# The sums of weights in a Strassen-like feed-forward block, made in the pair that uses them

## The reference, cut to what matters

```
x = x + mix @ w_out                      # rg_out in layer 0, sb_out in layer 1
h = rmsnorm(x, norm_ffn_g[layer])
g = h @ w_gate                           # 1024 x 2816
u = h @ w_up                             # 1024 x 2816
x = x + (silu(g) * u) @ w_down           # 2816 x 1024
```

## Time and profile before

| | |
|---|---|
| median of 3 runs | 1966.46 us (1963.02 to 1968.39) |
| the profiled execution | 1964.4 us, span 1962.7 us |
| TensorE busy | 1875.2 us, 96% of the span |
| VectorE busy | 1279.7 us, 65% |
| ScalarE busy | 951.7 us, 48% |
| mean granted TensorE clock | 0.988 |
| DMA | 208.64 MB, mean 106 GB/s |

### The profile page before, as it was taken

One profiled execution on the slowest core, in us unless ns is written; L12 is line 12 of the kernel. 1 busy time (PEld: TensorE's weight loads), 2 busy tenths in 40 slices (PEclk: granted clock), 3 DMA queues, 4 the chain that ended last, 5 costly groups with the idle time before them and its releaser, 6 DMA issues. The chain is left out here.

```text
span 1962.7 us, 30196 instructions
## 1 busy us (share of the span) xinstructions
PE 1875.2 (96%) x10662; PEld 1567.3 (80%) x10662; DVE 1279.7 (65%) x2220; ACT 951.7 (48%) x1573; POOL 233.6 (12%) x322
## 2 busy tenths in 40 slices
PE   9999888998899999988899899999999999999998
PEld 7787788888888777778898898876677887777777
DVE  7787767646765766677764676666677556556553
ACT  6576556325544444556632454345565344445442
POOL 3011111001100000011100110000001135341000
PEclk9999999999999999989999999999999999999999
DMA  7334566346532222256634653212222233232322
GB/s 253 104 97 129 144 154 153 103 122 167 123 106 75 66 64 64 65 149 152 150 108 120 165 123 120 76 54 59 62 84 76 94 88 89 75 91 75 96 82 74
DMA packets 79220, 208.64 MB, mean 106 GB/s; under 512 B 10209, under 2 KB 18529, under 8 KB 79121
## 3 DMA queue, kind: packets, MB, share of 16 engines
q1 hardware_dynamic: 60080, 174.16, 28.3%
q0 software_dynamic: 19040, 33.20, 9.7%
HBM read 203.12 MB, written 4.21 MB: 106 GB/s over the span
## 5 line engine op out<-in xcount | busy, mean ns | idle before, releaser
L642 PE MATMUL ps<-Hl,Wh 128*128 128x512 f32 x784 | 328.4, 419 | 0.0
L1340 ACT ACTIVATE Wh<-Wr 128x1024 fp32r<-128x1024 f32 (+2 forms) x172 | 195.6, 1139 | 257.4 <-PE ps L644 232.9
L644 PE MATMUL ps<-Hh,Wh 128*128 128x512 f32 x784 | 307.2, 392 | 0.0
L643 PE MATMUL ps<-Hh,Wl 128*128 128x512 f32 x784 | 306.4, 391 | 0.0
L1903 DVE TENSOR_TENSOR Wl<-Wr,Wh 128x1024 fp32r<-128x1024 f32 (+2 forms) x172 | 231.4, 1345 | 102.9 <-ACT Wh L1340 101.6
L642 PE MATMUL ps<-Yl,Wh 128*128 128x512 f32 (+1 forms) x648 | 253.9, 392 | 11.4 <-DVE Wl L1903 8.2
L643 PE MATMUL ps<-Yh,Wl 128*128 128x512 f32 (+1 forms) x648 | 250.4, 386 | 0.0
L644 PE MATMUL ps<-Yh,Wh 128*128 128x512 f32 (+1 forms) x648 | 250.2, 386 | 0.0
L728 PE MATMUL ps<-Hl,Wh 128*128 128x256 f32 x528 | 155.3, 294 | 58.2 <-DVE gs L2096 57.3
L642 PEld LDWEIGHTS ps<-Hl,Wh 128*128 128x128 f32 x784 | 147.4, 188 | 40.3 <-issue 11.3
L644 PEld LDWEIGHTS ps<-Hh,Wh 128*128 128x128 f32 x784 | 147.1, 188 | 32.9
(11 more groups left out here) (404 smaller groups left out, 4106.5 us busy)
## 6 DMA issues: line engine op xcount, KB each, us to landing
Wr<-in_w SPq DMA_DIRECT2D x162, 512.0 KB, 3.6
Wr<-in_w SPq DMA_DIRECT2D x32, 768.0 KB, 4.1
scr<-in_w SPq DMA_DIRECT2D x66, 256.0 KB, 3.3
Wr<-in_w SPq DMA_DIRECT2D x66, 256.0 KB, 3.0
scr<-in_w SPq DMA_DIRECT2D x22, 512.0 KB, 5.0
scr<-in_w POOLq DMA_DIRECT2D x44, 256.0 KB, 6.5
Wr<-in_w POOLq DMA_DIRECT2D x44, 256.0 KB, 5.7
Wr<-in_w SPq DMA_DIRECT2D x16, 640.0 KB, 3.8
```

The costliest lines, as they stand in the source:

```text
L642: pe.matmul(bank[:, 0:n], hi, rl[:, k, :], start=(k == 0), stop=False)
L643: pe.matmul(bank[:, 0:n], lo, rh[:, k, :], start=False, stop=False)
L644: return pe.matmul(bank[:, 0:n], hi, rh[:, k, :], start=False, stop=(k == kc - 1))
L1340: act.activation(place(Wh, slot, kc), place(Wr, slot, kc), ACT.Copy).then_inc(w_hi, 1)
```

## The change

Four things:

- `second_sum(g)` and `fourth_sum(g)` are made at the beginning of pair g (behind the rest of S4 of g-1 and behind the rest of S3 of g+1), where before those of g+1 were made in the middle and at the end of pair g.
- The cast and the rest of S2 of pair g are made in pair g, ahead of those of A of g+1, where before S2 of g+1 came last in pair g. Pair 0 keeps its place: its sums are made in `out_proj` and in the first iteration.
- `split_at` numbers the stream to match; the waits of SP, TensorE, ScalarE and VectorE that use it follow.
- In `out_proj` of `rg_out` and `sb_out`, at m = 3, 4 and 5, the rest of the weight two units on goes ahead of the row quarters, where before it came behind them.

```diff
 def split_at(h, pairs):
+    at = {"S3": 6 * h - 2, "A": 6 * h, "A22": 6 * h + 2, "S2": 6 * h + 5, "S1": 6 * h + 7, "S4": 6 * h + 9}
     if isinstance(h, int) and h == 0:
-        return {"S3": 1, "A": 2, "A22": 3, "S2": 4, "S1": 7, "S4": 10}
+        at.update(S3=1, A=2, A22=3, S2=4)
+    if isinstance(h, int) and h == 1:
+        at.update(S3=5)
     if isinstance(h, int) and h == pairs - 1:
-        return {"S3": 6 * h - 1, "A": 6 * h, "A22": 6 * h + 2, "S2": 6 * h + 3, "D0": 6 * h + 5, "S1": 6 * h + 6, "S4": 6 * h + 7}
-    return {"S3": 6 * h - 1, "A": 6 * h, "A22": 6 * h + 2, "S2": 6 * h + 3, "S1": 6 * h + 7, "S4": 6 * h + 10}
+        at.update(S2=6 * h + 4, D0=6 * h + 5, S1=6 * h + 6, S4=6 * h + 7)
+    return at
...
# ScalarE, ffn_in, iteration(g, par)
-                    used = {..., "S2": 6 * g + 3, "S4": 6 * g - 2}
+                    used = {..., "S2": 6 * g - 3, "S4": 6 * g - 2}
...
                     if drain:
                         return
+                    if n != 0:
+                        sum_hi(name, g, "S2", par, b + used["S2"])
                     if n == 0 and norm:
                         root(norm)
                     if more:
...
                     if more:
                         sum_hi(name, g + 1, "A22", 1 - par, b + used["A22"])
-                        sum_hi(name, g + 1, "S2", 1 - par, b + used["S2"])
...
# VectorE, out_proj
                     if name in ("rg_out", "sb_out") and m == 0:
                         split(u0 + 4, 0, KD)
+                    if pairs_in and nrm and 2 < m < 6:
+                        split(u0 + m + 2, m % 2, KD)
                     if pairs_in and nrm and m % 2 == 0:
                         even_quarters(nrm, m)
                     if pairs_in and nrm and m % 2:
...
-                    elif (m > 2 or name not in ("rg_out", "sb_out")) and m < 6 or not pairs_in:
+                    elif not nrm and m < 6 or not pairs_in:
                         split(u0 + m + 2, m % 2, kc_of(u0 + m + 2))
...
# VectorE, ffn_in, iteration(g, par)
                     if n != 0:
                         sum_lo(name, g - 1, "S4", 1 - par)
+                    if n != 0 and not drain:
+                        second_sum(name, g, par)
                     if n not in (0, 1) and not drain:
                         act_by_up(g - 2, par)
                     if more and n != 0:
                         sum_lo(name, g + 1, "S3", 1 - par)
+                    if n != 0 and not drain:
+                        fourth_sum(name, g, par)
                     if n not in (0, 1):
                         y_lo_ffn(g - 2, par)
...
                         sum_lo(name, 1, "S3", 1)
+                    else:
+                        sum_lo(name, g, "S2", par)
                     if more:
-                        second_sum(name, g + 1, 1 - par)
                         sum_lo(name, g + 1, "A", 1 - par)
...
-                    if more:
-                        fourth_sum(name, g + 1, 1 - par)
-                        sum_lo(name, g + 1, "S2", 1 - par)
```

More of the change, by code:

```diff
@@ L1441, in iteration @@
                     more = n is None or n + 1 < pairs
-                    used = {"S3": 6 * g - 1, "A": 6 * g, "S1": 6 * g + 1, "A22": 6 * g + 2, "S2": 6 * g + 3, "S4": 6 * g - 2}
+                    used = {"S3": 6 * g - 1, "A": 6 * g, "S1": 6 * g + 1, "A22": 6 * g + 2, "S2": 6 * g - 3, "S4": 6 * g - 2}
                     if n == 0:
-                        used = {"S3": 2, "A": 2, "S1": 0, "A22": 3, "S2": 4}
+                        used = {"S3": 2, "A": 2, "S1": 0, "A22": 3}
                     if n == 1:
-                        used["S4"] = 0
+                        used.update(S2=4, S4=0)
                     if last:
```

## The result

The changed kernel takes 1894.89 us, median of 4 runs (1893.74 to 1895.18), beside 1965.15 for the kernel before on the same chip (4 runs, 1963.02 to 1968.39). The ratio is 0.9641, 95% interval 0.9625 to 0.9656: faster by 3.6%. The prediction was 1890.5 us, range 1883 to 1908: the forecast case came true, 4.4 us above its number. The profiled execution took 1895.13 us, its span is 1893.5, where the kernel before had 1964.4 and 1962.7.

A forecast was written before the change was run, and what follows sets the result against it. A DMA leg and VectorE's in-order queue, closing in one turn of the pair loop, were taken as the bound: 1964.4 - 75.8 + 2.2 - 2.4 = 1888.4, given as 1890.5 since the runs' median is 2.1 higher; range 1883 to 1908.

The forecast's parts named there:

- the forecast case: Whole kernel: TensorE becomes the bound at 10.06 us a turn; 1890.5 us, alone spanning 1884 to 1898; chance 0.72.
- The loop and its new length: Gate/up pair loop through `sum1`: 12.32 us in one turn before, 15.6 us over two after, 7.8 a turn.
- VectorE's clock: Gate/up pair: VectorE's instructions timed from TensorE's S3 at 0, 8.2 us of work within 10.06, 0.6 us left over.
- the prediction's own sign of being wrong: Changed profile: TensorE waits for the rest of S2 or A, or accumulates land later than 7 us after issue.
- Gain 75.8: Four gate/up stretches: 439.0 us fall to 363.2, as 36 turns of 10.06 plus twice 0.5 us.
- 0.5 us for the norm: Pair 1 of the two norm stages: 0.5 us each for the norm's spread, added to the stretches.
- Loss 2.2: Stage ends: down's unit 0 loads later, costing 1.0 us in each of two stages, 0.1 in the others.
- Gain 2.4: Out-projection at m = 3: the weight's rest moves up 1.2 us, in two places; 0 to 8.2 possible.
- "0" for the quarters: Out-projection at m = 4 and 5: row quarters, now later, stay hidden behind TensorE's units, costing 0.
- its case: Pair loop: VectorE's row of waits becomes the bound; at 10.5 us a turn it loses 16 us: 1906; chance 0.14.
- The DMA case: Pair loop: the DMA leg still shows; an accumulate of 12 us gives 10.7 a turn, 1914; chance 0.08.
- the 19 us from which I had the change turn slower: Slower rival: leg through `sum1` must pass 19 us instead of 10.24; at 21 us, 2000; chance 0.04.

## Why the prediction was right, point by point

- **The loop and its new length: right.** The wait of 93.4 us is 0.6; the steady turn is 10.07 for 10.06. The 12.2 us a turn that the prediction set out from is an average that no usual turn had, pair 1 at 15 to 18.5 and the others at 11.6; the sum is not hurt by it, since it starts from the whole stretches. Taking the leg away (10.07 in the old order) and lengthening it (one turn pays all, two turns pay the excess) show the cause, not only its end.
- **VectorE's clock: right to 0.2 us.** From S3 at 1056.54: second sum 1.47 (1.6 predicted), fourth 3.27 (3.4), low part of Y 4.34 (4.4), the instruction behind S2's rest 5.89 (6.05), second read to 9.3 (9.4).
- **DMA: right for S1, wrong for S3.** S1: load at 8.08 (8.0), landing 17.0 (17.6), sum 21.61 (21.7). The load of S1 is slower than in the earlier trace rows and the accumulate faster (4.2 for 5.7), so that the leg kept its length while its parts changed. S3 was to land "within a microsecond of S1's"; it lands 4.4 us later in the turn shown, and 3.2 to 4.7 in most. Its accumulates take 7.4 us at the median where they took 6.5, so that the prediction's own sign of being wrong, accumulates that land later than 7 us after their issue, was there. That the time held all the same was partly luck: the 4 us of room are S1's alone, and the cast of S3 has half a microsecond at the median. The engines' share is 0.66 to 0.68, not 0.72; with the sums at the end of the pair before it is 0.69 to 0.72. Why stays open.
- **"Gain 75.8": 72.7.** The term that I mis-sized is pair 1 and pair 2 of the two norm stages. Pair 1's turn is 11.63 and 11.53, not 10.56. It also has two matmuls of 512 columns that no other pair has (0.46 us), a delay of about 0.5 at a read, and one of about 0.3 for the rest of S2, each followed by a few slower starts. Without the accumulate, in the order of before, it is 11.53 as well, so it is no DMA and none of the change's doing: I had 0.5 us for the norm where 1.5 were due. Pair 2 is 10.44 and 10.58, 0.4 and 0.5 us where I took 0 and had 1.4 as the bound; without the accumulate it is 10.07. Not the buffer that I looked at shows there: the second sum waits only 0.19 us and stands at 246.65. It is S3 of pair 3, whose late landing holds ScalarE, and through its cast VectorE's queue ahead of the rest of S2:

```profile
248.75 0.63 ACT L1377 ACTIVATE Fh<-scr 128x512 fp32r<-128x512 f32 x1 [1.07 <-DMA scr<-in_w]
```

  The prediction's own sum had less room there than it said, too: from 247.29, six instructions and the rest of S2 end at 251.3 by its start-to-start times, not at 250.8, with TensorE wanting it at 251.5.
- **"Loss 2.2": 4.2.** The mechanism is as put: load at 3.49 after S3 (3.5 predicted), TensorE idle for 1.04 and, at the third stage's end, 0.81. But I followed unit 0 alone. The load of unit 1 is later too (12.5 us after the last S3 for 10.8), its rest comes ahead of the right rows, and Y with it: another 0.5 us in each of the two longer stages. In the two shorter ones down's first matmul comes at 10.36 and 10.45 after the last S3, not 10.06, where I had put 0.1. With the last pair's sums made early all of it is gone from the first stage (87.27 for 89.00).
- **"Gain 2.4": 2.3 in the two profiled executions (2.22 and 0.12), and not to be told from 0 in the medians.** The idle at m = 3 fell by 1.3 at each place, as the edit says. The step that failed is "0" for the quarters: they are hidden at m = 4 and 5, but pair 0 waits for them, 1.34 us in `sb_out` where there was no wait, 1.29 in `rg_out` where there were 0.77. In `rg_out` the clock did not fall in this execution (below), as it did in that of before; how much of the 2.22 is the clock's stays open.
- **The sum.** 76.0 predicted (75.8 - 2.2 + 2.4), 69.3 measured between the two profiled executions. The 6.7 are: stretches 3.1, ends 2.0, units 0.1, and 1.7 ahead of anything edited, for which a prediction has no term.
- **The rivals.** VectorE had over 1.2 us to spare and less than 2.4; its case was further off than the 0.6 left over on my clock said. The DMA case was priced by the right formula but with a leg that grows only in the accumulate; in the kernel with two accumulates the load grows as well (4.59), and so the leg is dearer. A leg of 17.77 gave 1958, still under the kernel before: that fits the 19 us from which I had the change turn slower. VectorE without pauses (50.00 of 50.00) did not hold up POOL's issues, 0.88 us each at the median as before (0.87). By that, the trace agrees with the Trainium skill (SBUF — State Buffer, "Who interferes with whom"), which takes tensor_tensor for harmless to GpSimd's descriptors.

## What to carry to other kernels

Where an engine waits in its queue for a DMA although the DMA engines are half idle, write down the loop: from the instruction that frees the buffer, over load and accumulate, to the one that uses it, and through the queue back to the freeing one; the length of the loop by the turns that it spans is the bound. If it binds, move the waiting instruction to behind the instruction that frees the next buffer: any place will do between the landing and the use, and the latest is not the best, for what the moved instruction frees (here down's first load) moves along with it. After such a move, follow the next stage's first two loads, not only the first, and every other DMA that shares the queue: here S1's leg kept over 4 us of room and S3's, behind it, 0.5. And look at the first turns of such a loop by themselves: a third of the gain lay in four turns of 36.

## What the runs showed of the hardware

- **Two idle moments of nearly the same length, one with and one without a fall of the clock.** At the same unit of two stages of the kernel after, on its timeline of TensorE:

```profile
204.64 0.47 PE L645 MATMUL ps<-Yl,Wh 128*128 128x512 f32 x1 [2.78 <-DVE Wl L1907]
...
804.21 0.77 PE L645 MATMUL ps<-Yl,Wh 128*128 128x512 f32 x1 [2.86 <-DVE Wl L1907]
```

The 8 us behind each, by stretch:

```profile
204.64:212.64 8.00, 8.00 (x35) 6.61 (x36) 7.05 (x12) 4.63 (x6) 0.93 (x1) 1.00 0.83 263
804.21:812.21 8.00, 8.00 (x28) 6.53 (x29) 7.05 (x12) 4.29 (x6) 0.87 (x1) 0.79 0.72 222
```

Full speed in the first, a part of the time at 1.2 GHz in the second. Over all kernels of this study, this unit behind 4.08 to 4.18 us of idle had a mean clock of 0.62 to 0.81 in the 8 us after it in all of 8 places; behind 2.82 to 2.87 us 0.62 to 0.81 in all of 7; behind 2.77 or 2.78 us 0.79 to 0.82 in four and 1.00 in three; behind 2.17 and 2.23 us 1.00 in both. The first matmul alone doesn't tell it: in the kernel with the sums alone it took 0.47 us after 4.18 of idle, and the 8 us still have 0.79.

- **A DMA's time to landing depends on what else is in flight.** Leaving out S1's accumulate brings that of S3 from 6.5 to 4.6 us (medians of 44, both of 256 KB). The accumulate into S1 took 5.7 us at the median before and 4.2 after. As the second of two it took 4.1 in the order of before; in that of after it took 6.1, the longest 8.9. S1's load of 256 KB took 2.9 before and 4.3 after. The length of the turn is not what decides it: with the sums at the end of the pair before, in the same turn of 10.07, the load takes 3.0 and the accumulate 5.9. Which transfer delays which was not tested further. The lengths that I took from another order of loads are why my expectations for both experiments with two accumulates missed, one to each side.
